# Short convolution of the delta rule: the values' tiles on GpSimd instead of VectorE

## What is computed

```python
def causal_short_conv(x, w):
    width = w.shape[0]
    s = x.shape[1]
    xp = jnp.pad(x, ((0, 0), (width - 1, 0), (0, 0)))
    return sum(xp[:, i:i + s] * w[i] for i in range(width))
...
qkv = jax.nn.silu(causal_short_conv(jnp.concatenate([dn_q, dn_k, dn_v], axis=-1), dn_conv_w))
cq, ck, cv = jnp.split(qkv, 3, axis=-1)
```

## Time and profile before

| | us |
|---|---|
| three runs | 2856.29, 2851.55, 2855.61 |
| median | 2855.61 |
| profiled execution, its own time | 2856.84 |
| span of the profiled execution | 2855.0 |
| TensorE busy | 2718.2 (95%) |
| VectorE busy | 1388.8 (49%) |
| ScalarE busy | 556.3 (19%) |
| GpSimd busy | 8.7 |
| mean granted clock of TensorE | 0.975 of full speed |

### The profile page before, as it was taken

The page is one execution under the profiler, slowest core; times in us unless marked ns, Lnnn a source line. Parts: engine busy times, 40 slices in busy tenths (PEclk is TensorE's granted clock), DMA queues, the critical chain, the costliest instruction groups (busy, mean ns, idle before and its releaser), DMA issues.

```text
span 2855.0 us, 48678 instructions
## 1 busy us (share of the span) xinstructions
PE 2718.2 (95%) x19890; PEld 2435.1 (85%) x19890; DVE 1388.8 (49%) x2251; ACT 556.3 (19%) x1161; POOL 8.7 (0%) x19
## 2 busy tenths in 40 slices
PE   7999999999999999999999999899997899989999
PEld 6998768888999899776988899768996589966999
DVE  5554154323554655225521465426663456615765
ACT  2112132111111111123201111232112421123211
POOL 0000000000000000000000000000000000000000
PEclk9999999999999999997999999999998999999999
DMA  6654320234565555421123555423443134431442
GB/s 247 227 202 145 110 101 16 75 120 161 211 225 184 198 204 212 156 90 66 45 70 138 212 203 204 176 89 135 161 178 118 65 128 169 178 135 44 148 174 107
DMA packets 50169, 416.00 MB, mean 146 GB/s; under 512 B 4016, under 2 KB 4272, under 8 KB 29584
## 3 DMA queue, kind: packets, MB, share of 16 engines
q1 hardware_dynamic: 49344, 409.34, 38.9%
q0 software_dynamic: 592, 3.41, 0.3%
HBM read 411.69 MB, written 1.05 MB: 145 GB/s over the span
## 4 chain that ended last, share of the span: by engine, by line
PE 90%; DVE 4%; ACT 3%; issue 2%; DVEq 1%; ACTq 1%
PE units L733 29%; PE units L675 22%; PE spots L733 21%; PE spots L990 4%; PE spots L705 2%; PE units L1142 1%; PE units L1235 1%; PE units L804 1%; ACT squares L1303 1%; PE spots L714 1%; ACT probabilities L1303 1%; PE spots L1176 1%; PE units L1138 1%; PE spots L1166 1%; PE spots L1157 1%
## 5 line engine op out<-in xcount | busy, mean ns | idle before, releaser
L675 PE MATMUL units<-normed,weights 128*128 128x256 f32 x2016 | 452.8, 385 | 17.2 <-ACT normed L1303 14.2
L675 PEld LDWEIGHTS units<-normed,weights 128*128 128x128 f32 x2016 | 385.8, 193 | 79.9 <-issue 12.1
L733 PE MATMUL units<-normed,weights 128*128 128x128 f32 x2176 | 276.6, 281 | 22.2 <-DVE normed L1681 16.1
L733 PEld LDWEIGHTS units<-normed,weights 128*128 128x128 f32 x2176 | 262.1, 197 | 37.2 <-DVE normed L1681 18.6
L733 PE MATMUL spots<-normed,weights 128*128 128x128 f32 x2176 | 268.7, 277 | 0.0
L733 PEld LDWEIGHTS spots<-normed,weights 128*128 128x128 f32 x2176 | 257.9, 194 | 0.0
L1303 ACT ACTIVATE mla_q_rope<-units 128x256 f32<-128x256 f32 (+1 forms) x248 | 95.3, 387 | 591.0 <-PE units L733 553.5
L1796 DVE TENSOR_TENSOR delta_new_values<-spots,mla_q_rope 128x256 f32<-128x256 f32 x116 | 49.3, 425 | 277.4 <-PE spots L733 277.4
L733 PE MATMUL units<-hidden,weights 128*128 128x128 f32 x1472 | 180.9, 276 | 0.0
L733 PE MATMUL spots<-hidden,weights 128*128 128x128 f32 x1472 | 180.1, 275 | 0.0
L733 PEld LDWEIGHTS units<-hidden,weights 128*128 128x128 f32 x1472 | 172.0, 192 | 6.7 <-issue 6.7
(11 more groups left out here) (324 smaller groups left out, 3564.7 us busy)
## 6 DMA issues: line engine op xcount, KB each, us to landing
weights<-stream SPq DMA_DIRECT2D x140, 2048.0 KB, 7.7
values_mla_qk_mla_values<-stream SPq DMA_DIRECT2D x24, 2048.0 KB, 8.3
weights<-stream SPq DMA_DIRECT2D x46, 1024.0 KB, 5.2
weights<-stream SPq DMA_DIRECT2D x16, 768.0 KB, 5.3
constants<-consts SPq DMA_DIRECT2D x1, 1094.5 KB, 8.0
residual<-x_in SPq DMA_DIRECT2D x1, 1024.0 KB, 5.0
weights<-stream SPq DMA_DIRECT2D x4, 256.0 KB, 5.0
conv_in<-ctx_in POOLq DMA_DIRECT2D x1, 1024.0 KB, 5.4
```

The costliest lines, as they stand in the source:

```text
L675: mm = pe.matmul(dst, w[:, kt * width + col:kt * width + col + P], rhs[:, kt, :], start=(kt == 0), stop=(kt == k - 1))
L733: mm = pe.matmul(dst[:, m * P:m * P + P], weights[:, m, kt, :], moving(kt), start=(first and m == 0 and kt == 0), stop=(kt == n - 1), skip ...
```

## The change

The loop of `conv` on VectorE runs over 8 tiles instead of 12. GpSimd gets a new function, called once in each layer ahead of its wait for the norm: it waits until all of `conv_in` is there and makes the four value tiles in one piece of 128 x 1024 for each step, product and sum as separate instructions, with a drain behind each. ScalarE waits for both before SiLU.

```diff
+        conv_v_done = signal("conv_values_done", one=1)
...
+            def conv_values(c):
+                u = unit(c, "dv", 0)[0]
+                dst, tmp = qkv[:, 8:12, :], hT[:, 16:20, :]
+                pool.wait_ge(*taken(c, u))
+                pool.wait_ge(*taken(c, u + 1))
+                for tap in range(TAPS):
+                    w = vec[:, V_TAP + 12 * tap + 8:V_TAP + 12 * tap + 12].unsqueeze(2).to_broadcast([P, 4, T])
+                    ins = pool.tensor_tensor(dst if tap == 0 else tmp, conv_in[:, 8:12, tap:tap + T], w, ALU.mult)
+                    pool.drain()
+                    if tap:
+                        ins = pool.tensor_tensor(dst, dst, tmp, ALU.add)
+                        pool.drain()
+                ins.then_inc(conv_v_done.handle, 1)
+
             pool.dma_start(vec[:, :], vec1[0]).then_inc(vec_here.handle, 16)
             with pool.Fori(0, DEPTH - 1) as l:
+                conv_values(Place("one", l))
 
                 pool.wait_ge(*normed.at(Place("one", l), 3 * KD))
...
+            conv_values(Place("one", DEPTH - 1))
             pool.wait_ge(*normed.at(Place("one", DEPTH - 1), 3 * KD))
...
             def conv(c):
                 e_.wait_ge(*conv_done.at(c, 1))
+                e_.wait_ge(*conv_v_done.at(c, 1))
                 activate(qkv[:, :, :], qkv[:, :, :], ACT.Silu)
...
-                for m in range(12):
+                for m in range(8):
                     w = vec[:, V_TAP + 12 * tap + m:V_TAP + 12 * tap + m + 1]
```

## The result

The changed kernel takes 2868.3 us (median of six, 2865.9 to 2872.0) against 2856.5 us before (six, 2851.6 to 2857.5): a ratio of 1.0045, 95% interval 1.0032 to 1.0058, so 11.8 us slower by the medians. The forecast was 2875 us with a range of 2855 to 2891 and the sign slower. The profiled execution took 2867.8 us, its span is 2865.8 us.

The account below looks back on a forecast made before the run. The chain was taken as TensorE for 90%. Tap 3 10.6 us late, less 1.0 us coming back, gave 9.6 us a layer, 19.2 in two: from 2856.84 to 2876.0, less 1.2 for the median, 2875 us; range 2855 to 2891.

Parts of the forecast that it names:

- The mechanism: Convolution: GpSimd and VectorE alternate by instruction, delaying tap 1, L1849's copies and TensorE's dz; 9.6 us a layer lost.
- Rival 1: Convolution: no turns, GpSimd works beside VectorE, only tap 3's saving is seen: -3.2 us, 2852.4 us; chance 0.12.
- rival 2: Convolution: VectorE keeps going, GpSimd gets only stretches without two-input work, ScalarE waits 4.1 us a layer: 2864; chance 0.09.
- rival 3: Convolution: two-input GpSimd instructions cost 3.5 us, turns of 3.8 us, another 8.6 us a layer: 2892; chance 0.12.
- GpSimd's price: Values' convolution on GpSimd: 2.28 us for each product or sum, seven a layer make 16.0 us.
- The turns: Taps 0 and 1: one VectorE tap instruction in about 2.56 us, 17.9 us for seven in layer 0.
- the bound of 2870 us: Taps 0 and 1: two tap instructions slip through in each turn, tap 1 ends some 2.7 us earlier.
- The clock: TensorE after its wait ahead of dz: about 3.4 us of work at half speed, costing 1.7 us in layer 0.
- What came back at the squares' products: TensorE at L928: its 1.83 us wait goes and the half clock after it may not come, 1.0 us taken.
- The relief: Tap 3 on VectorE, ahead of SiLU: four fewer instructions save 1.6 us on the path, 3.2 us in two layers.

Follow-up runs that it names:

- e3: Changed kernel with tap 1 moved behind the copies of the MLA values in VectorE's order: 2859.6 us.
- e8: Changed kernel with 14 GpSimd memsets of 128x1024 a layer in place of products and sums, values' convolution left out: 2847.8 us.
- e4: Changed kernel with GpSimd starting only when both copies of the MLA values are made: 2866.2 us.
- e7: Changed kernel with GpSimd's products and sums done tile by tile, 28 instructions of 128x256 instead of seven of 128x1024: 2853.4 us.
- e5: Changed kernel with only GpSimd's four products, back to back without drains, into four places, the three sums left out: 2852.3 us.
- e1: Changed kernel without GpSimd's work: VectorE makes 8 tiles, the values' convolution is left out: 2847.3 us.
- e10: Against the kernel before: all twelve tiles on VectorE, taps 0 and 1 of queries and keys made in its earlier waiting, GpSimd idle: 2848.7 us.

## Why the prediction was right, and where its size was off

**The mechanism held step by step.** Instructions take turns, the delayed copies of L1849 stand behind tap 1, TensorE waits for their bank, the clock falls, ScalarE's new wait costs nothing. e3 shows the link from the copies to TensorE, e8, and e4 less cleanly, the exclusion by operands and not by tensor, e7 that the length of one instruction is the lever. Rival 1 fell with the first taps of 9.31 us, rival 2 with GpSimd's undisturbed 16.0 us, rival 3 with products of 1.9 us.

**GpSimd's price** was right: seven in 16.0 us, as taken; product 1.9 us, sum 2.34 to 2.48 us. By the Trainium skill (GPSIMD Engine Reference, Performance versus the Vector engine) an add of 1024 would be an estimated 2.25 us, half of its figure for 2048. The sums here lie 4 to 10% above it.

**The turns** were too long and too poor. I added 0.28 us of stretching to each, from copies that ran back to back; with a drain behind each instruction VectorE's short one fits in the gap, and a turn is 2.28 us. And two tensor_scalar went through in each (a case that I had kept as the bound of 2870 us; e5 shows the drain as the reason). Together tap 1 ends at 391.3 instead of 393.9, dz starts 2.4 us earlier than forecast, tap 3 ends at 407.75 instead of 410.1.

**The clock** behind dz cost 1.8 us in layer 0 (8.84 us against 7.07 for the products of dz) and 2.5 us in layer 1 (9.59), 1.7 was taken. What came back at the squares' products is 1.7 us (5.39 to 3.69), 1.0 was taken.

**Where the miss lies.** To see it, take from each profile the time from TensorE's first product for the turning of the queries (L919, ahead of dz) to its first product with the finished convolution (L949). All that the forecast counts happens between these two, once in each layer.

| profile | layer 0, us | layer 1, us | both, to before | whole span, to before |
|---|---|---|---|---|
| before | 41.65 | 42.89 | | |
| changed kernel | 49.03 | 50.16 | +14.7 | +10.8 |
| e1, relief only | 39.27 | 39.29 | -6.0 | -5.8 |
| e5, no drains, no sums | 41.86 | 42.05 | -0.6 | -5.9 |
| e7, short holds | 42.23 | 42.49 | +0.2 | -2.8 |
| e10, queries and keys early | 40.92 | 39.82 | -3.8 | -10.0 |

The forecast had 19.2 us, the stretches of the convolution show 14.7 us and the whole profile 10.8 us. The first 4.5 us of the miss come from the shorter turns and from what came back at the squares' products, less what the clock behind dz cost beyond 1.7 us. The other 3.9 us lie outside: falls of the granted clock that the kernel before has and the changed kernel has not, as from 1570 to 1612 in layer 1, less some that the changed kernel alone has of the two (3.3 us between 460 and 600). The forecast had no term for falls of the clock outside these stretches, and gave no reason for leaving them out. On balance it took the loss too high, by 7.4 us against the median of the runs' difference, and the range covers that.

**The relief.** "Of that 1.6 us, tap 3's, is on the path: 3.2 us in two layers." e1 measured 10.7 us by the medians. In the stretches of the convolution it has 6.0 us, the 3.2 us of tap 3 and the rest from the products of the squares (5.39 to 3.69 us in layer 0). What is beyond that goes with the granted clock elsewhere, and the shorter chain is not shown as its cause. e5 and e7 speak against it: with stretches about as long as before, to 1 us in two layers, they are 5.8 and 4.7 us faster by the medians. Why nearly every variant has fewer falls of the clock than the kernel before stays open.

## What to carry to other kernels

Before arithmetic is given to GpSimd, look at which VectorE instructions run beside it. Here scalar_tensor_tensor and tensor_scalar stood still for the length of each GpSimd product or sum, so a wide one (1.9 to 2.5 us) was worse than four narrow ones, and what stood behind them in VectorE's order paid. First see whether VectorE has a wait ahead of the work into which a part can be moved: here that gave 0.3 to 0.4% where the division lost 0.45%, though a part of this gain came with the clock, as in variants that moved nothing.

## What was not expected

- The same seven operations, cut in four, take the wait ahead of dz from 7.72 to 0.67 us, and the time from 11.8 us above the kernel before to 4.7 us below it (e7). The first explains why the loss is gone, not the gain.
- A drain behind a GpSimd instruction helps VectorE's short tensor_scalar: two a turn instead of one (e5).
- Variants that save next to nothing in the stretch of the convolution are 5.8 and 4.7 us faster than the kernel before (e5, e7). TensorE's granted clock stood at 0.83 and 0.72 before and at 1.00 in e1 and in the changed kernel alike, in stretches without any change. Differences of 0.1 to 0.4% between such kernels are not read from the path alone.
